# A norm's factor moved behind the products, rows between columns, and rank tiles that share a width

## The reference, cut to what matters

```
h  = ffn_half_step(h,  g_ffn1, m[0],  m[1],  m[2],  w13_ffn1, w2_ffn1)
hc = ffn_half_step(hc, g_ffn1, mc[0], mc[1], mc[2], w13_ffn1, w2_ffn1)
z  = modulate(rms_norm_2(h, g_mix), m[3], m[4]) @ w_in      # and the same of hc
...                                                          # mixers, output projection
h  = ffn_half_step(h,  g_ffn2, m[6],  m[7],  m[8],  w13_ffn2, w2_ffn2)   # hc too, but not in the last layer

def ffn_half_step(h, g, shift, scale, gate, w13, w2):
    return h + 0.5 * gate * swiglu(rms_norm_2(h, g) * (1 + scale) + shift, w13, w2)
def swiglu(x, w13, w2):
    a, b = split(x @ w13);  return (silu(a) * b) @ w2        # widths 1024 -> 2 x 2816 -> 1024
```

## Time and profile before

| | |
|---|---|
| median of three timed runs | 3552.52 us (3549.99 to 3560.23) |
| the profiled execution, its span | 3532.96 us, 3531.1 us |
| PE busy, of the span | 3226.1 us (91%), 16644 matmuls |
| PEld, DVE, ACT, POOL busy | 2658.7, 1687.7, 811.2, 46.6 us |
| granted TensorE clock, mean | 0.919 of 2.4 GHz |
| DMA | 27.0% of 16 engines, 80 GB/s read |

### The profile page before, as it was taken

How to read it: one execution, slowest core, us unless ns; L and a number is a source line. 1 busy time by engine, 2 the same in 40 slices (tenths; PEclk the granted TensorE clock), 3 DMA queues, 4 the chain that set the end, 5 groups by cost and what they waited for, 6 DMA issues and landing times. The chain is left out here.

```text
span 3531.1 us, 39881 instructions
## 1 busy us (share of the span) xinstructions
PE 3226.1 (91%) x16644; PEld 2658.7 (75%) x16644; DVE 1687.7 (48%) x2462; ACT 811.2 (23%) x1031; POOL 46.6 (1%) x32
## 2 busy tenths in 40 slices
PE   6867899699999979888999999799999988889998
PEld 5666566588888868566888888688888765668886
DVE  4823975455453554563443432554544455543334
ACT  2202223322111121322211212321111132232222
POOL 0400000000000000000000000000000000000000
PEclk8975577899999989988999999899999998899999
DMA  3330111343342312011333221233332221223331
GB/s 110 90 98 30 54 42 46 110 119 125 95 134 74 118 37 73 16 65 36 108 105 92 89 75 58 71 120 118 118 109 83 89 56 27 65 72 95 95 95 60
DMA packets 344426, 288.83 MB, mean 82 GB/s; under 512 B 21104, under 2 KB 319728, under 8 KB 343280
## 3 DMA queue, kind: packets, MB, share of 16 engines
q1 hardware_dynamic: 344304, 287.17, 27.0%
HBM read 280.31 MB, written 2.10 MB: 80 GB/s over the span
## 5 line engine op out<-in xcount | busy, mean ns | idle before, releaser
L1739 PE MATMUL PS<-x_hi_f,w_hi 128*128 128x512 f32 x2240 | 616.3, 344 | 6.2 <-DVE w_lo L1780 6.2
L1739 PE MATMUL PS<-x_hi_f,w_lo 128*128 128x512 f32 x2240 | 619.4, 346 | 0.0
L1739 PE MATMUL PS<-x_lo_f,w_hi 128*128 128x512 f32 x2240 | 616.1, 344 | 0.0
L1739 PEld LDWEIGHTS PS<-x_hi_f,w_hi 128*128 128x128 f32 x2240 | 354.9, 189 | 63.7 <-issue 7.5
L1739 PEld LDWEIGHTS PS<-x_hi_f,w_lo 128*128 128x128 f32 x2240 | 353.8, 188 | 53.3
L1739 PEld LDWEIGHTS PS<-x_lo_f,w_hi 128*128 128x128 f32 x2240 | 352.6, 188 | 54.5
L1790 DVE TENSOR_TENSOR hid_f_f<-PS,silu_a_f 128x768 f32<-128x768 f32 (+1 forms) x88 | 78.4, 891 | 652.5 <-ACT silu_a_f L1760 652.5
L1749 ACT ACTIVATE w_hi<-w_raw 128x2048 fp32r<-128x2048 f32 x131 | 250.0, 1908 | 513.9 <-PE PS L1739 505.8
L1739 PE MATMUL PS<-hid_hi_f,w_lo 128*128 128x512 f32 x1232 | 340.1, 345 | 0.0
L1739 PE MATMUL PS<-hid_hi_f,w_hi 128*128 128x512 f32 x1232 | 338.2, 344 | 0.0
L1739 PE MATMUL PS<-hid_lo_f,w_hi 128*128 128x512 f32 x1232 | 338.1, 344 | 0.0
(11 more groups left out here) (295 smaller groups left out, 4186.5 us busy)
## 6 DMA issues: line engine op xcount, KB each, us to landing
w_raw<-in_w_ffn_dram SPq DMA_DIRECT2D x240, 512.0 KB, 5.0
sq_f<-in_w_ada_dram SPq DMA_DIRECT2D x120, 512.0 KB, 3.5
w_raw<-in_w_in_dram SPq DMA_DIRECT2D x46, 512.0 KB, 4.7
ada_room<-in_w_ada_dram SPq DMA_DIRECT2D x24, 512.0 KB, 3.5
w_raw<-in_w_out_dram SPq DMA_DIRECT2D x24, 512.0 KB, 5.5
w_raw<-in_w_ffn_dram SPq DMA_DIRECT2D x32, 384.0 KB, 4.1
ada_s<-in_conditions_dram SPq DMA_DIRECT2D x4, 1024.0 KB, 4.9
hT<-hT SPq DMA_DIRECT2D x56, 64.0 KB, 2.0
```

What stands on the lines that cost most here:

```text
L1739: last = nc.tensor.matmul(c.PS[:, 4 * q + 2 * w + m, 0:e - a], wt, xt[:, a:e], start=first, stop=end)
```

## The change

Three edits.

**Feed-forward.** `Deferred` takes the place of `Normed` in `ffn`. The operand is `hT` times gain alone; the shift of each span is put beside the tokens as an extra column of x (in the one-span call twice), so that its product with the weights comes out as a column of the result. The token's factor is put on the products when they are evicted: DVE copies the shift's products (`shift_out`), multiplies a and b by `inv`, ACT takes silu with the shift's product as its bias, and DVE adds b's and multiplies. The norm's sums are made beside the first step: step 0 is written with all of w = 0 first, then PE makes the sums in banks of step 1, and step 1 waits for the root. The matmuls of an up step are cut in `pieces`: 512 and 258 columns in the wide calls, 256 and 258 in the last (512 before). Down steps keep their spans. `ada`'s first loads come behind the third step's weights.

**First projection.** The 14 steps run in the order `FIRST_STEPS`, rows between columns. **Rank tiles.** The 96 columns of each half of the query rank stand in one tile of 128 with the 32 rope columns, plain in one and swapped in the other; the four tiles of 96 become two, and nine tiles seven.

```diff
+FIRST_STEPS = "cccrcrcrcrccrr"
...
-                if i < n_col:
+                if not chunk[i]:
...
+class Deferred(Operand):
...
+        self.shifts = shifts * 2 if len(spans) == 1 else shifts
+        self.hi, self.lo = sb(f"x_hi_{tag}", [P, KT, n + v], F32R), sb(f"x_lo_{tag}", [P, KT, n + v], F32R)
+        self.sq, self.inv = sb("sq_" + tag, [P, 4, n]), sb("inv_" + tag, [P, n])
...
+    def scalar(self, act, meanwhile):
+        nc, b = self.c.nc, self.b
+        for v, s in enumerate(self.shifts):
+            nc.scalar.activation(self.hi[:, :, self.n + v], s, ACT.Copy)
+        for k in range(KT):
+            for (a, e), g in zip(self.spans, self.gains):
+                last = nc.scalar.activation(self.hi[:, k, a:e], self.c.hT[:, k, a:e], ACT.Identity, scale=g[:, k:k + 1])
+            last.then_inc(self.rounded.sem, 1)
+        meanwhile()
+        for k in range(KT):
+            if k >= 4:
+                act.wait_ge(self.added.sem, b[self.added] + k - 4)
+            if k == 4:
+                act.wait_ge(self.added.sem, b[self.added] + 1)
+            nc.scalar.activation(self.sq[:, k % 4, :], self.c.hT[:, k, 0:self.n], ACT.Square).then_inc(self.squared.sem, 1)
+
+    def root(self, act, bank):
+        act.wait_ge(self.summed.sem, self.b[self.summed] + 1)
+        for a, e in self.spans:
+            last = self.c.nc.scalar.activation(self.inv[:, a:e], self.c.PS[:, bank + a // 512, 0:e - a], ACT.Sqrt, bias=self.c.eps[:])
+        last.then_inc(self.rooted.sem, 1)
+
+    def sums(self, pe, bank):
+        pe.wait_ge(self.added.sem, self.b[self.added] + KT - 1)
+        for a, e in self.spans:
+            last = self.c.nc.tensor.matmul(self.c.PS[:, bank + a // 512, 0:e - a], self.c.ones[:], self.inv[:, a:e], start=True, stop=True)
+        last.then_inc(self.summed.sem, 1)
+
+    def vector(self, dve, ch, meanwhile):
+        nc, b = self.c.nc, self.b
+        for k in range(KT):
+            dve.wait_ge(self.rounded.sem, b[self.rounded] + k + 1)
+            if k == 0:
+                for v, s in enumerate(self.shifts):
+                    nc.vector.tensor_tensor(self.lo[:, :, self.n + v], s, self.hi[:, :, self.n + v].bitcast(F32), ALU.subtract)
+            for (a, e), g in zip(self.spans, self.gains):
+                last = nc.vector.scalar_tensor_tensor(self.lo[:, k, a:e], self.c.hT[:, k, a:e], g[:, k:k + 1],
+                                                      self.hi[:, k, a:e].bitcast(F32), ALU.mult, ALU.subtract)
+            last.then_inc(self.ready.sem, 1)
+        meanwhile()
+        for k in range(1, KT):
+            dve.wait_ge(self.squared.sem, b[self.squared] + k + 1)
+            if k > 1:
+                dve.wait_ge(self.added.sem, b[self.added] + k - 1)
+            so_far = self.sq[:, 0, :] if k == 1 else self.inv[:]
+            nc.vector.tensor_tensor(self.inv[:], so_far, self.sq[:, k % 4, :], ALU.add).then_inc(self.added.sem, 1)
+
+    def invert(self, dve, ch):
+        dve.wait_ge(self.rooted.sem, self.b[self.rooted] + 1)
+        ch.link(self.c.nc.vector.reciprocal(self.inv[:], self.inv[:]))
...
+    cut = 512 if wide else 256
+    pieces = [(0, 0, cut), (1, cut, n_tok + n_sh)]
...
-                x.wait(sp, KT - 1)
-                share.load(sp, 0)
...
+                            if s == s0 + 2:
+                                sp.wait_ge(x.summed.sem, x.b[x.summed] + 1)
+                                share.load(sp, 0)
...
+            def up_products(i):
                 q = (s0 + i) % 2
                 pe.wait_ge(ring.split, s0 + i + 3)
                 for w in range(2):
-                    whi, wlo = up[0][q][:, w, k, :], up[1][q][:, w, k, :]
-                    for wt, xt, first, end in ((whi, hi, k == 0, False), (whi, lo, False, False), (wlo, hi, False, k == KT - 1)):
-                        for m, (a, e) in enumerate(spans):
-                            last = nc.tensor.matmul(c.PS[:, 4 * q + 2 * w + m, 0:e - a], wt, xt[:, k, a:e], start=first, stop=end)
-                return last
-
-            x.tensor(pe)
-            opening(x, pe, products_of, lambda i, last: last.then_inc(ring.used, 1))
+                    for k in range(KT):
+                        if i == 0 and w == 0:
+                            x.wait(pe, k)
+                        whi, wlo = up[0][q][:, w, k, :], up[1][q][:, w, k, :]
+                        for wt, xt, first, end in ((whi, hi, k == 0, False), (whi, lo, False, False), (wlo, hi, False, k == KT - 1)):
+                            for m, a, e in pieces:
+                                last = nc.tensor.matmul(c.PS[:, 4 * q + 2 * w + m, 0:e - a], wt, xt[:, k, a:e], start=first, stop=end)
+                last.then_inc(ring.used, 1)
+
+            up_products(0)
+            x.sums(pe, 4 * ((s0 + 1) % 2))
+            pe.wait_ge(x.rooted.sem, x.b[x.rooted] + 1)
+            up_products(1)
...
-                        act.wait_ge(ring.used, s + 3)
-                        act.wait_ge(ring.drained, s + 1)
-                        nc.scalar.activation(sa[:, q, :], res(q, 0), ACT.Silu).then_inc(silu_done.sem, 1)
-                        act.wait_ge(ring.drained, s + 3)
+                        act.wait_ge(scaled.sem, 2 * i + (f0 + k + sc0 + 1))
+                        for v, (a, e) in enumerate(spans):
+                            last = nc.scalar.activation(sa[:, q, a:e], sa[:, q, a:e], ACT.Silu, bias=cc[:, q, 0, v:v + 1])
+                        last.then_inc(silu_done.sem, 1)
+                        act.wait_ge(made.sem, 2 * i + (f0 + k + mk0 + 1))
...
+            x.root(act, 4 * ((s0 + 1) % 2))
...
+                        dve.wait_ge(ring.used, s + 3)
+                        nc.vector.tensor_copy(cc[:, q], c.PS[:, 4 * q + 1:4 * q + 4:2, n_tok - cut:n_tok - cut + n_sh])
+                        nc.vector.tensor_tensor(paired(sa[:, q, :]), up_res(q, 0), paired(x.inv[:]), ALU.mult).then_inc(scaled.sem, 1)
+                        nc.vector.tensor_tensor(paired(hf[:, q, :]), up_res(q, 1), paired(x.inv[:]), ALU.mult).then_inc(ring.drained, 1)
                         dve.wait_ge(silu_done.sem, u + (u0 + 1))
-                        nc.vector.tensor_tensor(hf[:, q, :], res(q, 1), sa[:, q, :], ALU.mult).then_inc(ring.drained, 1)
+                        dve.wait_ge(ring.drained, s + 3)
+                        for v, (a, e) in enumerate(spans):
+                            last = nc.vector.scalar_tensor_tensor(hf[:, q, a:e], hf[:, q, a:e], cc[:, q, 1, v:v + 1], sa[:, q, a:e],
+                                                                  ALU.add, ALU.mult)
+                        last.then_inc(made.sem, 1)
...
+            x.invert(dve, c.dve.on(dve))
...
-KR_AT = OFF_KR - QK_NOPE
-
-
 def kv_tiles(dram, l):
-    return [(OFF_KV, P), (KR_AT, QKW), (0, QKW, dram["w_kr_swapped"][l])]
-
-
-REST_TILES = [(OFF_Q, 96), (OFF_Q + 96, 96), (OFF_F, P), (OFF_F + P, P), (OFF_P, P), (OFF_P + P, P)]
+    return [(OFF_KV, P), (0, P, dram["w_q_kr"][l, 0]), (0, P, dram["w_q_kr"][l, 1])]
+
+
+REST_TILES = [(OFF_F, P), (OFF_F + P, P), (OFF_P, P), (OFF_P + P, P)]
...
-                        return nc.vector.tensor_copy(krT[QK_NOPE:QKW, tile - 1, a:e], ps[QK_NOPE:QKW])
+                        if e <= n_out:
+                            nc.vector.tensor_copy(cqT[:, tile - 1, a:e], ps[0:96])
+                        return nc.vector.tensor_copy(krT[QK_NOPE:QKW, tile - 1, a:e], ps[96:P])
...
-                    x = Normed(c, sb, spans, [mod(v, m + 1) for v in vs], [mod(v, m) for v in vs], f"f{l}{half}")
+                    x = Deferred(c, sb, spans, [mod(v, m + 1) for v in vs], [mod(v, m) for v in vs], f"f{l}{half}")
```

98 lines of the change are left out of this document (62 added, 36 removed).

## The result

The changed kernel takes 3461.98 us (median of four runs, 3452.90 to 3465.77) against 3551.26 (3545.42 to 3560.23) before: a ratio of 0.974, 95% interval 0.9714 to 0.9766, faster. Its profiled execution took 3452.90 us (span 3451.1), 80.0 us less than that of before; the prediction's sum said 82.2.

The account below looks back on a forecast made before the run. The prediction took the feed-forwards as PE-bound outside their openings. Gains of 52.6, 11.3, 27.5 and 8.0 us less losses of 13.4, 2.4 and 1.4 made 82.2 us: 3450.8 us profiled, 3470 median, range 3446 to 3502.

Parts of the forecast that it names:

- Fronts: Feed-forward openings: step 2 starts earlier with the norm beside step 0; 52.6 us gained in three wide, 11.3 in the fourth.
- rival B: Feed-forward openings: the wait at the root replaces the old one, 27 us lost, 3497 us; chance 0.1.
- The split: Fourth feed-forward's up steps: 256 + 258 columns cost 14 ns more a product, 13.4 us lost.
- Rival C: Fourth feed-forward: a split product costs only its columns by the skill page's rule, 3460 us; chance 0.05.
- Two columns in the wide steps: Wide feed-forwards' up steps: two more columns cost 0.83 ns a pair, 2.4 us lost.
- rival A: Wide feed-forwards: the pair's pace tips, all slow 3493 us or all fast 3459; chance 0.17 for the slow one.
- The longer chain: Up steps: the chain from last product to hidden lo grows from 3.7 to 5.5 us; 1.4 us lost over four feed-forwards.
- Rank tiles: Second block's input projection: two tiles for four save a two-tile step in each layer, 27.5 us gained.
- First projection: First projection: the mixed order of column and row steps gains 8 us, bounds 13 and -3.
- the term on the clock: First projection: the 156-column chunk, no longer after a wait, leaves half clock; 10 us gained.
- Rival D: Feed-forward up steps: the odd operand with 258-wide pieces makes the kernel slower than before, 3880 us at worst; chance 0.03.
- E: First projection: the new order gives nothing or loses 3 us, 3478 to 3481 us in all; chance 0.1.

Follow-up runs that it names:

- E6: The kernel before the change, run again unchanged as a single execution: 3548.34 us.
- E10: The changed kernel with PE making the norm's sums ahead of step 0's products instead of behind them, a single execution: 3520.32 us.
- E7: The changed kernel without the extra shift columns and without the split in the last feed-forward, operand rows kept at 770 and 514, shift left out: 3455.63 us.
- E11: The changed kernel with the edits of E4 and E8, and x rows of 784 in the wide and 768 in the last feed-forward: 3445.56 us.
- E9: The kernel before with x rows of 770 (514 in the last feed-forward), only addresses changed, a single execution: 3554.67 us.
- E2: The changed kernel with the query and key rank tiles apart again, nine column tiles: 3491.83 us.
- E4: The changed kernel with the first projection's sums a quarter instead of half a step behind a column step: 3453.28 us.
- E8: The changed kernel with the last feed-forward in two parts, its other 18 up steps in one piece on a normed second buffer: 3466.22 us.

## Why the prediction was right, step by step

The forecast of 3470.0 stands 8 us above the median and the range holds it. That is not all skill. The sum was good to 2 us on the profiled executions, and it was so because errors made up for each other: the four gains came out 5.6 us larger than forecast, the losses of the steady parts 6.9 us larger. The other 10 us or so lie in the distance from profiled execution to median, 19.6 us before and 9.1 after. The first trace of before was a quick one: E6, the same kernel with one slow and two fast feed-forwards as well, took 15.4 us more, 12.1 of them in the attention and 3.1 in the first projection. Such a distance is a draw of one execution and could not carry over as a constant.

1. **Fronts: right, for the reason given.** Step 2 at 41.2, 41.8, 41.3 and 28.5 us against 42.4, 41.5, 42.4 and 29.4. Its 5 us at half clock stood for 2.5 us lost in step 0; the wide ones' step 0 took 18.3, 19.4 and 18.3 us for 16.7 us of products, so 1.6 to 2.7. The root's wait is 1.1 us in the wide ones and 0.8 in the last; rival B did not come. E10 shows the mechanism.
2. **The split: a price that holds where the operand lies as before, and a term for the layout that is missing.** 768 split products take 91.7 us in the trace after, 119.4 ns each and 238.8 a pair where 226.7 stood: 12.1 ns, 11.6 us over 960. Another 3.0 us of the fourth steady part are its down steps, 232.4 ns a product (192 in 44.6 us) instead of 226.7 (192 in 43.5).

```profile
3140.60:3185.20 44.60, 44.60 (x194) 36.19 (x193) 16.19 (x15) 8.92 (x6) 0.00 (x0) 1.00 0.34 96
3185.20:3276.90 91.70, 91.70 (x770) 91.67 (x769) 39.36 (x45) 24.06 (x22) 0.00 (x0) 1.00 0.31 90
```

   But the 12.1 ns hold two causes. With the rows of 514 kept and the split taken away, 384 products take 89.1 us, 232.0 ns each (E7, the first row below), so there the split costs 6.8 ns. With rows of 768, 96 split matmuls take 11.5 us, 120.0 ns each by their starts and 240.0 a product (E11, the last feed-forward's third step, the second row): 13.3 ns over 226.7, near the forecast's 14.

```profile
3194.70:3283.80 89.10, 89.10 (x386) 72.24 (x385) 38.82 (x45) 24.06 (x22) 0.00 (x0) 1.00 0.31 89
```

```profile
3067.40:3078.90 11.50, 11.50 (x98) 11.50 (x97) 9.17 (x13) 5.27 (x6) 0.00 (x0) 1.00 0.60 165
```

   So the 15.0 us lost in the fourth steady part are 8.1 of layout (E9, 337.6 to 345.7), which the prediction had at nothing, and 6.3 of split (E7 to the changed kernel, 346.3 to 352.6), which it had at 13.4; that 13.4 came near 15.0 is in part chance. Rival C falls even so. The Trainium skill ("TensorE: Matmul & The Clock Gate", Wait — 56ns, not 53.3ns?) gives a fixed cost of about 2.5 ns a matmul; by it the split would cost an estimated 3.2 us, and no run here shows that.
3. **Two columns in the wide steps: wrong.** They cost 0, not 2.4 (E7). What was lost there, 9.1 us in the two traces, is rival A in another form: the rows of 770 put x and the hidden tiles elsewhere, and the pair takes 351.1 to 351.6 ns in each feed-forward and execution, between the 346.7 and 353.3 of before (E6, E9). Its sign hangs on the draw of before that it is set against: three feed-forwards at 346.7 would make it a loss of 19 us, three at 353.3 a gain of 10.
4. **The longer chain: 0.9 us of waits in all, not 1.4.** DVE has the cover that the prediction named.
5. **Rank tiles: 28.2 for 27.5**, by the mechanism given; E2 gives the step back.
6. **First projection: the sum came true (10.1 for 8.0), and the term on the clock by luck.** The stalls of 2.5 to 2.9 us stayed, as forecast, and E4 shows that the place of the sums makes them. The 10 us of the 156-column chunk are there only in executions that drop the clock in the old order, three of four here. Set against an execution like E9's (188.6 us from first to last product, 188.4 after) the change gives nothing. A fair term would have been 10 with a chance beside it.

Rival D (an odd operand slows) fell with the first window: the wide steady parts are at 523.5 us. E (nothing from the first projection) fell too, but in an execution like E9's it would have been nearly true.

What stays open is how an address sets the pace. From the starts of 192 pairs, a wide down step took 346.7 or 353.3 ns a pair with rows of 768, always 351.1 with 770 and 353.3 with 784. In the last feed-forward a 512-column product took 226.7 ns where every row and every tensor behind it is a whole number of KB, and 231.9 to 234.3 where x has rows of 514. It is the place and not a tensor's own row length alone: in E8 the second buffer has rows of 512 and lies 128 bytes and a small tile further, and it is the slowest; the hidden tiles too only moved. No run varied one tensor's place by itself.
